# VectorE's order in two stages of a fused two-layer kernel: branch weights ahead of modulation products, and modulation products four steps earlier

## The chip, the cores and the metric

The kernel runs on one core of a Trainium2 chip. The metric is the device time of one execution in microseconds; the kernel before takes 3525.2 us in the median of 3 runs (3522.25 to 3526.55). A profiled execution stands beside them, and all times inside the kernel are from it.

## The reference

Two layers of different kinds follow each other on 1024 tokens of width 1024, in float32. Layer one: RMS norm, an input projection, neighbourhood attention, a recurrent branch with gates, a gated mix of the two branches, and an MLP with a squared ReLU. Layer two is a modulated layer with window attention and a gated delta rule; its norms are scaled and shifted by vectors that come from a small product:

```
# layer one, end
mixed = sigmoid(g_att) * y_att + sigmoid(g_rec) * y_rec      # y_att = att @ w_att_o, y_rec = rec @ w_rec_o
x = x + mixed @ w_out[l]
h2 = rms_norm(x, ln2_g[l])
x = x + square(relu(h2 @ w_ff1[l])) @ w_ff2[l]
x = rms_norm(x, lnf_g)
# layer two, start
mod   = silu(c)     @ w_ada + b_ada                           # w_ada: 1024 x 6144
mod_c = silu(c_ctx) @ w_ada + b_ada
sh1, sc1, gt1, sh2, sc2, gt2 = split(mod, 6)
h = rms_norm_2(x, g_norm1) * (1 + sc1) + sh1
```

The change touches only the computation of `mod` and `mod_c`, which depends on nothing in layer one and is therefore done beside layer one's work, and the weights of `y_att` and `y_rec`.

## The kernel before

Every engine runs a program written out by hand, and semaphores tie them. Nothing reorders the instructions: each engine takes them as they are written. Large products are done in three matmuls each, because an operand is held as a high half and a low half: ScalarE copies the high half (L954 for the branch weights, L472 for the gate weights, L1539 for the MLP entries), and VectorE subtracts it from the plain values to get the low half (L959, L477, L1543).

**Modulation.** w_ada is cut into 12 groups of 512 columns, each of 8 blocks of 128 rows. VectorE multiplies a block by the vector's values and adds it up (`vector_mod`: L1395 for the first block of a group, L1398 for the others); groups 0 to 3 are done for two vectors, so 16 instructions, the rest for one, so 8. TensorE then sums the partitions with matmuls of one column (`tensor_mod`, L1418), and VectorE adds the bias (`vector_mod_out`, L1405). Groups 0 to 7 lie in the gate stage, groups 8 to 11 in the down product of layer one's MLP.

**Gate stage (`tensor_mix1`, `scalar_mix1`, `vector_mix1`).** Sixteen jobs x; in pass x TensorE computes the gates of job x (two halves of 24 matmuls), then the branch product of job x-1, then the column sums of modulation group x-1 (for the first eight). ScalarE applies the tanh to the gates (L1020), then splits off the high half of the gate weights for the next job and of the branch weights for job x-1. VectorE, for job x: bias column, modulation products of group x, low half of the branch weights, then the two evacuations (L1107) with the low half of later gate weights (L477) between them. Loads of w_ada blocks go three deep through SyncE, in one queue with the weights.

**Down product (`tensor_ff7` from `ORDER7`, `vector_ff7`, `sync_ff7`).** Layer one's MLP is done as seven products in the way of Strassen. The second half has 7 products of 16 steps, 112 steps u; a step is 12 matmuls with one block of hidden rows and one block of weights. Both are entries split by ScalarE and VectorE (L1539, L1543) in a ring of eight, so these run at most four steps ahead. For each step VectorE takes, in this order: an evacuation of the product before (`vector_taken`, L2014), a sum of weights for two steps on (`total`, L1890), the two low halves, and `vector_between`, where `it` is u-4 and the modulation products stand. SyncE brings the hidden rows in blocks of four steps (`rows(r)`, block r for steps 4r to 4r+3, issued when VectorE has done the first low half of step 4r-5), the weight pieces (`stream`), the two loads of X that the evacuations add to, and w_ada in pairs of blocks through four places (`sync_mod_pair`, pair y for products 2y and 2y+1, counted from the first of group 8). From the fifth on, a pair is issued when the products have left its place. `MOD_AT` says before which step TensorE makes the column sums of which group.

Of the kernel before, what the change touches and what calls it, by code (L numbers as in the profile page):

```python
# [131 lines left out]
def build(nc, d, out):  # L132
    ctx = ExitStack()
    with ctx:
# [58 lines left out]
        def R(off, n):  # L193
            return A[:, off:off + n]
# [279 lines left out]
        def vector_weights(e, x):  # L474
            o = 2048 * (x % 2)
            e.wait_ge(*m2_hi.at(split_at(x)))
            e.tensor_tensor(RR[:, o:o + 1024], MG[x % 2], RR[:, o + 1024:o + 2048].bitcast(F32),  # L477
                            ALU.subtract).then_inc(*m2_lo.tick())
# [447 lines left out]
        def branch_place(x):  # L926

            if x < 8:
                o = 1024 * (x % 2)
                return 20480 + o, TMP[:, o:o + 512], 4  # L930
            return (20480, TMP[:, 0:1024], 8) if x % 2 == 0 else (47104, YD[:, 0:1024], 8)
# [24 lines left out]
        def vector_branch(e, x):  # L956
            o, raw, kt = branch_place(x)
            e.wait_ge(*yd_hi.at(x + 1))
            e.tensor_tensor(RR[:, o:o + kt * 128], raw, RR[:, o + kt * 128:o + kt * 256].bitcast(F32),  # L959
                            ALU.subtract).then_inc(*yd_lo.tick())  # L960
# [10 lines left out]
        def vector_rec_lo(e, h):  # L971
            c = slice(h * 512, h * 512 + 512)
            for kk in range(8):
                e.wait_ge(*h_hi.at(h_lo.n + 1))
                e.tensor_tensor(RCL[:, kk, c], RC(kk, c), RCH[:, kk, c].bitcast(F32), ALU.subtract).then_inc(*h_lo.tick())
# [72 lines left out]
        def vector_mixed_lo(e, i):  # L1048
            kk, h, cols = unit_tile(i)
            e.wait_ge(*h_hi.at(16 + i + 1))  # L1050
            e.tensor_tensor(MXL[:, kk, cols], mixed_in(0, kk, h), MXH[:, kk, cols].bitcast(F32),
                            ALU.subtract).then_inc(*h_lo.tick())
# [9 lines left out]
        def vector_outw(e, name, i):  # L1062
            raw, lo, hi = OUTW[name]
            e.wait_ge(*m2_hi.at(outw_at(name, i)))
            e.tensor_tensor(RR[:, lo + i * 1024:lo + i * 1024 + 1024], raw[:, i * 1024:i * 1024 + 1024],
                            RR[:, hi + i * 1024:hi + i * 1024 + 1024].bitcast(F32), ALU.subtract).then_inc(*m2_lo.tick())
# [15 lines left out]
        def vector_mix1(e):  # L1082
            for u in range(32):
                x, h = divmod(u, 2)
                tt = tmpx[u % len(tmpx)]
                key = ("mo",) + mixed(x, h)
                ps, c, m, h = key[1:]
                dst = mixed_in(ps, c * 4 + m, h)
                if h == 0 and x < 8:
                    if x:  # L1090
                        vector_mod_out(e, x - 1)
                    for z in range(8 * x, 8 * x + 8):
                        vector_mod(e, z)
                if u == 17:
                    vector_mod_out(e, 7)
                if h == 0 and x and x not in (8, 15):
                    vector_branch(e, x)
                if u == 29:
                    vector_branch(e, 15)
                for i in MIXED_LO.get(u, ()):  # L1100
                    vector_mixed_lo(e, i)
                if u == 30:
                    for i in range(4):
                        vector_outw(e, "wo0", i)
                e.wait_ge(*bk.full(key))
                e.wait_ge(*bk.clear(("mg",) + key[1:]))
                e.scalar_tensor_tensor(out=tt if ps % 2 else dst, in0=tt, scalar=1.0, in1=bk.tile(key)[:, :],  # L1107
                                       op0=ALU.add, op1=ALU.mult).then_inc(*bk.emptying(key))
                if h == 0 and x + 2 < 16:
                    vector_weights(e, 24 + x + 2)  # L1110
                if u == 15:
                    vector_rec_lo(e, 0)
                    vector_branch(e, 8)
                    vector_rec_lo(e, 1)
            for i in (14, 15):
                vector_mixed_lo(e, i)
# [234 lines left out]
        mod_rows = lambda g: 2 if g < 4 else 1  # L1351
        acc_of = lambda g, b: R(47104 + 512 * b, 512) if g < 8 else R(51200 + g % 2 * 512, 512)
        pair_place = lambda y: (20480, 21504, 49152, 50176)[y % 4]
        MOD_AT = {22: 8, 30: 9, 38: 10, 46: 11}

        def raw_of(z):
            if z < 64:
# [18 lines left out]
        def sync_mod_pair(e, y):  # L1376
            g, kk = divmod(64 + 2 * y, 8)
            if y >= 4:
                e.wait_ge(*m_part.at(64 + 2 * y - 6))
            elif y == 0:  # L1380
                e.wait_ge(*bk.clear(("m3", 0, 15)))
            e.dma_start(R(pair_place(y), 1024).rearrange("p (k n) -> p k n", k=2),
                        d["w_ada"][kk * 128:kk * 128 + 256, g * 512:g * 512 + 512].rearrange("(k p) n -> p k n", p=P)
                        ).then_inc(*l_x[y % 4].tick())

        def vector_mod(e, z):
            g, kk = divmod(z, 8)
            e.wait_ge(*raw_there(z))
            if kk == 0 and (1 <= g < 8 or g >= 10):
                e.wait_ge(*bk.full(("md", g - 1 if g < 8 else g - 2)))  # L1390
            for b in range(mod_rows(g)):
                acc, scale = acc_of(g, b), sc3[:, kk, b:b + 1]
                last = b == mod_rows(g) - 1
                if kk == 0:
                    ins = e.tensor_scalar(acc, raw_of(z), scale, None, ALU.mult)  # L1395
                else:
                    e.wait_ge(*(m_part if last else dv).now())
                    ins = e.scalar_tensor_tensor(out=acc, in0=raw_of(z), scalar=scale, in1=acc, op0=ALU.mult, op1=ALU.add)  # L1398
                ins.then_inc(*(m_part if last else dv).tick())

        def vector_mod_out(e, g):
            key = ("md", g)
            e.wait_ge(*bk.full(key))
            for b in range(mod_rows(g)):
                ins = e.tensor_tensor(mods[:, b * 48 + g * 4:b * 48 + g * 4 + 4], bk.tile(key)[:, b * 4:b * 4 + 4],  # L1405
                                      V("bada", g * 4, 4), ALU.add)
            ins.then_inc(*bk.emptying(key))
# [51 lines left out]
        def seven(blk):  # L1459
# [131 lines left out]
            def tensor_ff7(e):  # L1591
# [22 lines left out]
                for pi, i in enumerate(ORDER7):  # L1614
# [4 lines left out]
                    for kts, ts in groups:  # L1619
                        if blk == 0 and 16 * pi + kts[0] in MOD_AT:  # L1620
                            tensor_mod(e, MOD_AT[16 * pi + kts[0]])
                        for t in ts:
# [411 lines left out]
            def sync_ff7(e):  # L2034
# [78 lines left out]
                    keep(KEEP2, t)  # L2113
                for r in range(4, 28):
                    rows(r)
                    if blk == 0 and r == 4:
                        for y in range(4):
                            sync_mod_pair(e, y)
                    if r == 4:
                        for k in range(2):  # L2120
                            e.wait_ge(*hidden_out(14 + k))
                        for h in range(2):
                            e.dma_start(X[:, 4 * h:4 * h + 4, :], x_of(xs)[:, 4 * h:4 * h + 4, :]).then_inc(*l_x3[h].tick())
                    if r < 26 and ORDER7[(r + 2) // 4] in STREAMED:
                        stream(ORDER7[(r + 2) // 4], (r + 2) % 4)
                    if blk == 0 and 5 <= r < 11:
                        for y in (2 * r - 6, 2 * r - 5):
                            sync_mod_pair(e, y)
                    if blk == 0 and r == 15:
                        e.wait_ge(*bk.full(("md", 11)))  # L2130
                        e.dma_start(lnf, row("lnf")).then_inc(*l_lnf.tick())
                        e.dma_start(Cx, d["ctx_2"].rearrange("(t p) n -> p t n", p=P)).then_inc(*l_c.tick())
# [86 lines left out]
                                       op1=ALU.mult).then_inc(*z_x.tick())  # L2219

        def vector_between(e, it):
            if 12 <= it < 44:
                vector_mod(e, 64 + it - 12)
            if it in (25, 33, 41, 49):
                vector_mod_out(e, 8 + (it - 25) // 8)
            if it == 50:
                vector_gains(e)
            k = it - 96
            if k == 2:
                vector_norm_mean(e, "nc")  # L2230
            if k == 4:
                vector_norm_factor(e, "nc")
                vector_norm_rows(e, "nc", 2, 0)
            if k == 8:
                vector_last_mean(e, 0)
            if k in (10, 11):
                e.wait_ge(*f_sm.now())
                vector_last_rows(e, 0, range(2 * k - 20, 2 * k - 18))
# [1736 lines left out]
```

## Time and profile before

| | |
|---|---|
| median of 3 runs | 3525.2 us (3522.25 to 3526.55) |
| profiled execution | 3526.55 us, its span 3524.7 us |
| mean granted TensorE clock | 0.964 |
| TensorE busy | 3289.8 us, 93% of the span |
| VectorE busy | 2275.9 us, 65% |
| ScalarE busy | 1465.9 us, 42% |

A span is the time from the first to the last instruction. Engines are named PE (TensorE), DVE (VectorE), ACT (ScalarE), POOL (GpSimd) and SPq (SyncE's queue of DMA issues). A timeline row reads: start, length, engine, line, operation, what is written and read, the number of instructions merged into it, and in brackets how long the engine stood idle before it and what released it. The DMA's issue rows end with the time from issue to landing.

### The profile page before, as it was taken

To read this page: it belongs to the slowest core of one execution; us is meant where nothing else is said; L and a number is where in the kernel's file an instruction comes from. 1 tells how busy PE (TensorE), PEld (TensorE's weight loads), DVE (VectorE), ACT (ScalarE), POOL (GpSimd) and SP (SyncE) were. 2 spreads that over 40 slices of the span, in tenths; PEclk is the share of its full clock that TensorE was granted. 3 is DMA by queue.
4 is the path that set the end of the run, shared out by engine and by line. 5 is a ranking of instruction groups with operands and counts; after the bars stand their busy time and mean duration, and the time that the engine had idled before them with its cause. 6 is when DMAs were issued, how large, how long until landed. Compare 5 with 4: busy or idle time off the path is not lost. (4 is left out here: it accounts for less than half of the span.)

```text
span 3524.7 us, 49737 instructions
## 1 busy us (share of the span) xinstructions
PE 3289.8 (93%) x19066; PEld 2531.6 (72%) x19066; DVE 2275.9 (65%) x3919; ACT 1465.9 (42%) x2690; POOL 572.1 (16%) x377
## 2 busy tenths in 40 slices
PE   7999998999999999999985776999999999999999
PEld 6767777887778887776554665646788657888887
DVE  4176997513498858786567886459422149885887
ACT  3176771212355443354434554218411035544443
POOL 1081000011134420010000000105201123442000
PEclk9999999999999999999997887999999999999999
DMA  3101115413144486553002122300022313447454
GB/s 135 44 3 31 45 36 159 129 50 114 60 138 149 152 308 209 193 185 135 4 15 42 36 46 59 108 18 2 19 54 69 105 48 123 164 152 278 148 196 157
DMA packets 311173, 363.20 MB, mean 103 GB/s; under 512 B 68660, under 2 KB 218100, under 8 KB 306460
## 3 DMA queue, kind: packets, MB, share of 16 engines
q1 hardware_dynamic: 309180, 352.95, 30.1%
q10 hardware_dynamic: 1760, 7.08, 0.9%
q8 instruction: 154, 2.52, 0.3%
q14 instruction: 79, 0.65, 0.1%
HBM read 269.38 MB, written 88.77 MB: 102 GB/s over the span
## 5 line engine op out<-in xcount | busy, mean ns | idle before, releaser
L96 PE MATMUL ps<-halves 128*128 128x512 f32 x4304 | 1007.3, 394 | 14.5 <-DVE halves L403 5.2
L96 PEld LDWEIGHTS ps<-halves 128*128 128x128 f32 x4304 | 811.6, 190 | 189.1 <-issue 10.1
L1586 PE MATMUL ps<-halves 128*128 128x512 f32 x2736 | 630.0, 393 | 9.5 <-DVE halves L1687 7.4
L1632 PE MATMUL ps<-halves 128*128 128x512 f32 x2688 | 616.3, 391 | 9.2 <-DVE arena L2014 5.5
L1586 PEld LDWEIGHTS ps<-halves 128*128 128x128 f32 x2736 | 518.4, 190 | 120.5 <-DVE halves L1687 8.3
L1632 PEld LDWEIGHTS ps<-halves 128*128 128x128 f32 x2688 | 505.7, 189 | 117.9 <-DVE arena L2014 7.4
L1539 ACT ACTIVATE halves<-raws 128x512 fp32r<-128x512 f32 x324 | 202.1, 630 | 446.1 <-PE ps L1632 307.7
L1543 DVE TENSOR_TENSOR halves<-raws,halves 128x512 fp32r<-128x512 f32 x324 | 268.9, 840 | 126.9 <-ACT halves L1539 126.0
L96 PE MATMUL ps<-arena 128*128 128x512 f32 (+1 forms) x800 | 315.1, 554 | 4.7 <-ACT arena L2784 3.0
L96 PEld LDWEIGHTS ps<-arena 128*128 128x128 f32 x800 | 151.9, 191 | 161.3 <-issue 152.4
L96 PE MATMUL ps<-arena,tokens 128*128 128x512 f32 (+1 forms) x384 | 140.4, 523 | 0.3 <-DMA tokens<-h_stash 0.3
L695 POOL TENSOR_SCALAR arena<-arena,sm 128x512 f32<-128x512 f32 x64 | 99.4, 1566 | 149.5 <-DVE sm L660 149.5
L1020 ACT ACTIVATE arena<-ps,hb 128x512 f32<-128x512 f32 x32 | 21.9, 688 | 233.5 <-PE ps L96 224.6
L96 PEld LDWEIGHTS ps<-arena,tokens 128*128 128x128 f32 x384 | 72.5, 191 | 62.7 <-issue 59.3
L1543 DVE TENSOR_TENSOR halves<-down_sums,halves 128x512 fp32r<-128x512 f32 x160 | 109.5, 684 | 0.0
L1661 ACT ACTIVATE staged<-staged 128x512 f32<-128x512 f32 x124 | 76.8, 620 | 75.6 <-DVE staged L1805 32.0
L1239 DVE SCALAR_TENSOR_TENSOR arena<-arena,ps 128x512 f32<-128x512 f32 x32 | 22.0, 686 | 129.0 <-PE ps L96 128.7
L2885 DVE TENSOR_TENSOR arena<-arena 64x30 f32<-64x30 f32 (+5 forms) x300 | 98.4, 328 | 10.0
L2888 DVE TENSOR_TENSOR arena<-arena 64x30 f32<-64x30 f32 (+5 forms) x300 | 97.8, 326 | 10.3
L1539 ACT ACTIVATE halves<-down_sums 128x512 fp32r<-128x512 f32 x160 | 98.6, 616 | 0.4 <-DVE down_sums L1890 0.4
L2025 POOL TENSOR_TENSOR staged<-staged 128x512 f32<-128x512 f32 x32 | 42.2, 1317 | 333.5 <-ACT staged L1663 333.5
L3576 POOL TENSOR_SCALAR arena<-arena,wst 128x640 f32<-128x640 f32 (+1 forms) x32 | 74.9, 2342 | 113.1 <-DVE wst L3536 113.1
(371 smaller groups left out, 4440.8 us busy)
## 6 DMA issues: line engine op xcount, KB each, us to landing
hidden_rows<-staged SPq DMA_DIRECT2D x32, 1792.0 KB, 5.8
raws<-hidden_rows SPq DMA_DIRECT2D x56, 1024.0 KB, 5.2
mixw<-in_w_in SPq DMA_DIRECT2D x56, 512.0 KB, 3.9
arena<-in_w_ada SPq DMA_DIRECT2D x64, 256.0 KB, 2.9
raws<-in_w_ff SPq DMA_DIRECT2D x32, 512.0 KB, 5.3
arena<-in_w_ff SPq DMA_DIRECT2D x16, 1024.0 KB, 7.4
raws<-in_w_mlp SPq DMA_DIRECT2D x32, 512.0 KB, 5.5
arena<-in_w_mlp SPq DMA_DIRECT2D x16, 1024.0 KB, 7.4
```

The costliest lines, as they stand in the source:

```text
L96: ins = e.matmul(out_ap, l, r, start=i == 0, stop=i == n - 1)
L695: e.tensor_scalar(pbuf[i % 5], pbuf[i % 5], c[:, 2:3], None, ALU.mult).then_inc(*a_sl.tick())
L1239: e.scalar_tensor_tensor(out=tt if ps % 2 else dst, in0=tt, scalar=1.0, in1=bk.tile(key)[:, :], op0=ALU.add, op1=ALU.mult).then_inc(*bk.em ...
L1539: e.activation(entry_part(x, 0), entry_source(x), ACT.Copy).then_inc(*f_wh.tick())
L1543: e.tensor_tensor(entry_part(x, 1), entry_source(x), entry_part(x, 0).bitcast(F32), ALU.subtract).then_inc(*f_ws.tick())
L1586: ins = e.matmul(o[:, :], l[:, k, :], r[:, k, :], start=first and k == 0 and i == 0, stop=last and k == 3 and i == 2)
L1632: ins = e.matmul(banks[t][:, :], l, r, start=kt == 0 and j == 0, stop=kt == 15 and j == 2)
L1661: e.activation(dst, dst, ACT.Relu).then_inc(*f_fh.tick())
L2025: e.tensor_tensor(staged(n, 5), staged(n, 3), staged(n, 7), ALU.add).then_inc(*f_sq.tick())
L2885: e.tensor_tensor(T3, bc(W3[:, k:k + 1, k + 1:32], [64, k, 31 - k]), bc(W3[:, 0:k, k:k + 1], [64, k, 31 - k]), ALU.mult).then_inc(*dv.tick())
L2888: e.tensor_tensor(W3[:, 0:k, k + 1:32], W3[:, 0:k, k + 1:32], T3, ALU.add).then_inc(*(i_sol if k == 30 else dv).tick())
L3576: e.tensor_scalar(p, p, w4[i % 4][:, 6:7], None, ALU.mult).then_inc(*w_sl.tick())
```

## The change

Two edits. In `vector_mix1` the low half of the branch weights (`vector_branch`, L959) is taken before the bias column and the modulation products of its job. In the down product the modulation products, their column sums, the bias columns and the gains (`vector_gains`) stand four steps earlier, and SyncE's issue of the pairs is rearranged: none ahead of the loads of X, and two behind each of the row blocks 4 to 11.

```
@@ vector_mix1
+                if h == 0 and x and x not in (8, 15):
+                    vector_branch(e, x)
                 if h == 0 and x < 8:
                     if x:
                         vector_mod_out(e, x - 1)
                     for z in range(8 * x, 8 * x + 8):
                         vector_mod(e, z)
                 if u == 17:
                     vector_mod_out(e, 7)
-                if h == 0 and x and x not in (8, 15):
-                    vector_branch(e, x)
@@
-        MOD_AT = {22: 8, 30: 9, 38: 10, 46: 11}
+        MOD_AT = {18: 8, 26: 9, 34: 10, 42: 11}
@@ sync_ff7
                 for r in range(4, 28):
                     rows(r)
-                    if blk == 0 and r == 4:
-                        for y in range(4):
-                            sync_mod_pair(e, y)
                     if r == 4:
                         for k in range(2):
                             e.wait_ge(*hidden_out(14 + k))
...
-                    if blk == 0 and 5 <= r < 11:
-                        for y in (2 * r - 6, 2 * r - 5):
+                    if blk == 0 and 4 <= r < 12:
+                        for y in (2 * r - 8, 2 * r - 7):
                             sync_mod_pair(e, y)
@@ vector_between
-            if 12 <= it < 44:
-                vector_mod(e, 64 + it - 12)
-            if it in (25, 33, 41, 49):
-                vector_mod_out(e, 8 + (it - 25) // 8)
-            if it == 50:
+            if 8 <= it < 40:
+                vector_mod(e, 64 + it - 8)
+            if it in (21, 29, 37, 45):
+                vector_mod_out(e, 8 + (it - 21) // 8)
+            if it == 46:
                 vector_gains(e)
```

VectorE in the gate stage, around the products of group 1 (L1395 and L1398), between two evacuations (L1107):

```order
 L477 TENSOR_TENSOR halves<-mixw,halves 128x1024
 L1107 SCALAR_TENSOR_TENSOR valw<-arena,ps 128x512
+L959 TENSOR_TENSOR halves<-tmps,halves 128x512
 L1405 TENSOR_TENSOR mods<-ps,vec 128x4 x2
 L1395 TENSOR_SCALAR arena<-arena,sc 128x512 x2
 L1398 SCALAR_TENSOR_TENSOR arena<-arena,sc 128x512 x14
-L959 TENSOR_TENSOR halves<-tmps,halves 128x512
 L1107 SCALAR_TENSOR_TENSOR valw<-arena,ps 128x512
```

L959 moved over the bias column and sixteen products; the same happens in jobs 2 to 7.

SyncE in the down product, from the last weight piece that is kept; raws are the blocks of rows 4 and 5, arena<-x_stash the loads of X. Before:

```order
L2078 DMA kept<-in_w_ff 128x4x512 x2
L2061 DMA raws<-hidden_rows 128x4x512
L1382 DMA arena<-in_w_ada 128x2x512 x4
L2123 DMA arena<-x_stash 128x4x1024 x2
L2061 DMA raws<-hidden_rows 128x4x512
L1382 DMA arena<-in_w_ada 128x2x512 x2
```

And now, where L2120 is the line that was L2123:

```order
L2078 DMA kept<-in_w_ff 128x4x512 x2
L2061 DMA raws<-hidden_rows 128x4x512
L2120 DMA arena<-x_stash 128x4x1024 x2
L1382 DMA arena<-in_w_ada 128x2x512 x2
L2061 DMA raws<-hidden_rows 128x4x512
L1382 DMA arena<-in_w_ada 128x2x512 x2
```

The first two pairs moved behind the loads of X, and the next two behind row block 5.

TensorE at the first column sums of the down product (L1418; L1632 are its steps, 12 matmuls each):

```order
 L1572 MATMUL ps<-identm,arena 128x128 x32
 L1586 MATMUL ps<-halves 128x512 x1320
-L1632 MATMUL ps<-halves 128x512 x264
+L1632 MATMUL ps<-halves 128x512 x216
 L1418 MATMUL ps<-onec,arena 128x1 x4
 L1632 MATMUL ps<-halves 128x512 x96
```

They moved from behind 22 steps to behind 18.

## Rows read from the trace of the kernel before

**Rows 1.** The page, busy time and share of the span by engine.
```profile
PE 3289.8 (93%) x19066; PEld 2531.6 (72%) x19066; DVE 2275.9 (65%) x3919; ACT 1465.9 (42%) x2690; POOL 572.1 (16%) x377
```

**Rows 2.** The timeline of TensorE in the gate stage.
```profile
571.30 1.84 PE L1418 MATMUL ps<-onec,arena 128*128 128x1 f32 x16
573.00 11.19 PE L96 MATMUL ps<-halves 128*128 128x512 f32 x48
...
592.30 11.19 PE L96 MATMUL ps<-halves 128*128 128x512 f32 x48
...
628.70 16.63 PE L96 MATMUL ps<-halves 128*128 128x512 f32 x72
...
645.98 16.63 PE L96 MATMUL ps<-halves 128*128 128x512 f32 x72
```

**Rows 3.** The waits of 515 to 850 us (total, times, longest).
```profile
PE ps L96 <- DVE halves L959: 1.6, 2, 0.9
```

**Rows 4.** The timeline of VectorE in the gate stage.
```profile
553.31 0.87 DVE L1395 TENSOR_SCALAR arena<-arena,sc 128x512 f32<-128x512 f32 x2
...
564.05 0.69 DVE L959 TENSOR_TENSOR halves<-tmps,halves 128x512 fp32r<-128x512 f32 x1
568.78 0.69 DVE L1107 SCALAR_TENSOR_TENSOR valw<-arena,ps 128x512 f32<-128x512 f32 x1 [4.04 <-PE ps L96]
...
628.96 0.49 DVE L1395 TENSOR_SCALAR arena<-arena,sc 128x512 f32<-128x512 f32 x1
...
637.84 0.69 DVE L959 TENSOR_TENSOR halves<-tmps,halves 128x512 fp32r<-128x512 f32 x1
```

**Rows 5.** The timeline of ScalarE in the gate stage.
```profile
562.16 0.62 ACT L954 ACTIVATE halves<-tmps 128x512 fp32r<-128x512 f32 x1
...
580.32 0.62 ACT L954 ACTIVATE halves<-tmps 128x512 fp32r<-128x512 f32 x1
```

**Rows 6.** The timeline of TensorE, the first twenty down steps.
```profile
1269.04 54.56 PE L1632 MATMUL ps<-halves 128*128 128x512 f32 x240
```

**Rows 7.** The timeline of VectorE in down steps 12, 16 and 20.
```profile
1296.36 0.68 DVE L1543 TENSOR_TENSOR halves<-kept,halves 128x512 fp32r<-128x512 f32 x1
...
1306.47 0.48 DVE L1395 TENSOR_SCALAR arena<-arena,sc 128x512 f32<-128x512 f32 x1
...
1319.64 0.69 DVE L2014 TENSOR_TENSOR arena<-arena,ps 128x512 f32<-128x512 f32 x1 [4.25 <-DMA arena<-x_stash]
```

**Rows 8.** Windows: length, busy (count) per engine, PEclk, DMA share, GB/s.
```profile
543.30:557.00 13.70, 7.42 (x26) 6.58 (x27) 12.01 (x21) 0.07 (x1) 0.00 (x0) 0.50 0.63 186
...
1366.00:1369.40 3.40, 3.40 (x8) 2.22 (x9) 1.90 (x3) 0.26 (x1) 0.00 (x0) 0.50 0.97 354
...
1293.00:1320.00 27.00, 27.00 (x121) 22.36 (x120) 13.11 (x21) 9.24 (x16) 0.00 (x0) 1.00 1.04 396
```

**Rows 9.** The timeline of TensorE, around three waits and column sums.
```profile
1332.47 1.02 PE L1418 MATMUL ps<-onec,arena 128*128 128x1 f32 x8 [2.38 <-DVE arena L1398]
...
1365.87 17.02 PE L1632 MATMUL ps<-halves 128*128 128x512 f32 x66 [2.75 <-DVE arena L2014]
...
1405.45 0.94 PE L1418 MATMUL ps<-onec,arena 128*128 128x1 f32 x8
```

**Rows 10.** The timeline of SyncE's queue in row block 4.
```profile
1292.80 5.55 SPq L1382 DMA_DIRECT2D arena<-in_w_ada  x4
1298.45 3.80 SPq L2123 DMA_DIRECT2D arena<-x_stash  x2
```

**Rows 11.** DMA issues at 1292.8 and at 1299.8 (KB, us to landing).
```profile
arena<-in_w_ada SPq DMA_DIRECT2D x1, 512.0 KB, 11.7
...
arena<-x_stash SPq DMA_DIRECT2D x1, 2048.0 KB, 19.8
```

**Rows 12.** DMA issues of 1320 to 1430 us (KB, median us to landing).
```profile
raws<-hidden_rows SPq DMA_DIRECT2D x9, 1024.0 KB, 6.0
...
arena<-in_w_ada SPq DMA_DIRECT2D x10, 512.0 KB, 3.9
```

## The prediction

> **What bounds the kernel now.** I read the page first: TensorE is busy for 93% of the span [rows 1], so nearly all that makes it wait is added to the end, and what runs beside it is free until it makes it wait. Then I read the timelines of two stretches, engine against engine, because the edit moves VectorE work in both: the gate stage (16 passes, 540 to 860 us) and the first block's down product (from 1269 us).
>
> In the gate stage TensorE's pass is 48 matmuls of gates, 24 of the branch product (twice as many from the ninth branch on) and the column sums of the modulation (L1418). The timeline shows gates starting at 573.00 and 592.30, a pass of 19.3 us while products have two rows, and at 628.70 and 645.98, 17.28 us, once they have one [rows 2]. The view of waits has TensorE waiting twice for the low half of the branch weights (L959), 1.6 us in all [rows 3]. VectorE has room: behind its products and L959 it stands idle for 4.0 us until the branch product is full [rows 4].
>
> The reader should see one more thing there. ScalarE makes the high half of the branch weights (L954) behind its tanh, and that tanh waits for the gates of the *next* pass: with gates from 573.00, L954 runs from 580.32 to 580.94, 7.9 us into TensorE's pass [rows 2, 5]. VectorE's products fill just these 8 us today.
>
> In the down product a step is 12 matmuls; 20 steps take 54.56 us, 2.73 each [rows 6]. The step numbers on VectorE come from its first product, L1395 at 1306.47, which belongs to step 16; four pairs of L1543 earlier, the one that ends at 1297.04 is step 12's [rows 7]. VectorE runs at most four steps ahead of TensorE, as an entry's slot is free only when the entry eight back is used.
>
> **Part 1: L959 ahead of the products.** It removes two TensorE waits, 1.6 us. It moves one instruction of 0.69 us over 9 or 17 others, and with it a wait: VectorE executes in order, so the bias column (L1405), the products and all behind them (evacuation L1107, weight halves L477) now stand behind ScalarE's L954.
> Pass x=1: L954 ends at 562.78 [rows 5]; L959 takes 0.7, L1405 0.15 and the 16 products, 553.31 to 564.05, 10.7 [rows 4]: they end at 574.3. The column sums that began at 571.30 [rows 2] begin at 574.4: +3.1 us.
> Passes x=2 and 3: counted from the gates' start, the products end at 7.9 + 0.7 + 0.15 + 10.8 = 19.6. Then come 1.7 us of column sums, and beside them L1107 (0.6) and L477 (1.2), which the next gates need: 21.5 against 19.3, +2.2 each, +4.4.
> Passes x=4 to 7: eight products take 8.9 (628.96 to 637.84) [rows 4]; 7.9 + 0.7 + 0.1 + 8.9 = 17.6, and L1107, L477 and 0.1 of latency make 19.5 against 17.28: +2.25 each, +9.0.
> The plain waits sum to 16.5 us, the 1.6 saved already inside. The loads of w_ada are issued as products free their places, so they move with them and the groups keep their length.
>
> To this comes TensorE's clock. The windows show it full (1.00, that is 2.4 GHz) while TensorE works without a gap, and half (0.50, 1.2 GHz) over 543.3 to 557.0, where it had stopped for the first products [rows 8]. The 2.75 us wait before 1365.87 is followed by 3.4 us at 0.50, in which 1.7 us are lost; the 2.38 us wait before 1332.47 is followed by no such stretch [rows 8, 9]. A two-row pass would now hold 3 us of wait and 1.7 of column sums of one column each; a one-row pass 1.1 of wait, 0.8 of sums and 1 more of wait. Bounds for a pass: 0 and 1.7 us. I take the drop after all three of the first kind and half of the other four, 5 x 1.7 = 8.5, less 1 that falls into waits: 7.5. Part 1 comes to +24 us. The Trainium skill (TensorE: Matmul & The Clock Gate, What's actually happening) says that the throttled state is the default and activity releases it. Read strictly, all seven passes would pay, 12 us in place of 7.5. The trace agrees that a stop is paid for afterwards, but it has one wait that costs and one that doesn't.
>
> **Part 2: modulation products four steps earlier.** VectorE's work is unchanged: 32 products of 0.66 us in steps 12 to 43, where they stood in 16 to 47. Steps 44 to 47 become 0.66 us lighter, where TensorE doesn't wait; the 2.75 us wait in step 32 is for evacuations (L2014) whose place is unchanged, and stays [rows 9]. So the move brings little by itself, and what counts is when the data are there. SyncE now issues both 2 MB loads of X first and behind them two w_ada pairs in place of four ahead of them; later, the pair for step 4r-4 goes out right behind block r of rows, and that one when VectorE has done the first subtraction of step 4r-5. The pair thus leaves one step before its use, where it was seven or more.
>
> The first pair: from 1293 to 1320 the DMAs move 396 GB/s with all engines busy [rows 8], 2.6 us for 1 MB, and they land in the order of issue: the pair issued at 1292.80 takes 11.7 us (1304.5), the last load of X, issued at 1299.8, takes 19.8 (1319.6), where VectorE goes on [rows 7, 10, 11]. Of these 6 MB, 5 now stand up to the second pair's end: it lands at 1317.0, the first at 1315.7. Bounds: 1304.5, its landing now, and 1319.6, behind everything; I take 1315.7 for the order seen. TensorE ends step 12 at 1304.5 (1269.04 + 13 x 2.73), and step 13's halves are ready at 1315.7 + 0.4 + 1.2 = 1317.3: it waits 12.8 us.
>
> Then come turns of four steps. From the issue of the rows to the landing of the pair behind them: a pair lands in 3.9 us in the median, 1 MB ahead of it adds 2.6: 6.5 us. Bounds 3.9 (not held up) and 7.3 (the rows' own median 6.0 and 1.3 for the half MB) [rows 12]. Blocks 10 and 11 have a 1 MB weight piece between: 9.1. From the landing to the next issue VectorE does its product (0.66), two steps (a pair of L1543 1.2, a product 0.66, with an evacuation or sum another 0.6) and the third's head: 5.0 us with pairs and products alone, 6.8 with the 0.6 in each. TensorE's four steps take 10.9.
> So from 1315.7: +4.7 = 1320.4, where block 5 leaves; +6.5 + 5.0 = 1331.9; twice +6.5 + 6.8 = 1358.5; +6.5 + 6.0 = 1371.0; +6.5 + 6.8 = 1384.3; +9.1 + 6.8 = 1400.2; +9.1 and 8.0 for the last four products = 1417.3. There the last column sums can start, ahead of step 42. Today they start at 1405.45 ahead of step 46 [rows 9], so step 42 began at about 1394.5. That is +23 us; the 2.38 us that TensorE now loses before 1332.47 lies inside. Drops of the clock after the long waits at steps 13 and 32, less those of before, add 1: +24 us.
>
> The Trainium skill (DMA: Bandwidth & Descriptors, Two DMAs through the same engine are not ordered) says that nothing orders DMAs across the 16 engines. If small pairs overtook the 2 MB loads here, the first rival below would hold. The landings seen don't show it: they come in the order of issue.
>
> **Sum.** 24 + 24 = 48 us on the profiled execution of 3526.55 us (span 3524.7). The median of the runs lies 1.35 lower: 3525.2 + 48 = 3573 us. Nothing later that I found starts at a fixed time, so I let nothing be given back.
>
> **Rivals.**
> *The data come in time; part 1 alone.* The first pair lands at 1304.5 and the others in 3.9 us. Then TensorE waits 1.6 us at step 13, a turn is 3.9 + 6.8 = 10.7, just under its 10.9, and part of the 2.38 us goes: about 0, and 3525 + 24 = 3549 us. For it: the 3.9 us row. Against: each pair stands behind at least 1 MB.
> *Slack covers part 1; part 2 alone.* If L954 were ready 3 us earlier, the products would end when TensorE arrives; 3549 us again. Against it: L954 follows the gates in both passes shown.
> *Faster, as it looks on paper.* L959 no longer holds TensorE (-1.6), and products one turn earlier end the 2.38 us wait: 3521 us. It is decided at one point in each part: L954 must be there when VectorE reaches it (553.3 in pass 1, and it is 9.5 us later), and the first pair by 1297.04.
> *SyncE's queue.* With full rings four w_ada issues took 5.55 us [rows 10]. If each of 7 turns pays 2 us for issuing, that adds 14, and the clock drops in all seven passes, +4: 3591 us.
>
> **Numbers.** The forecast has 62%, part 1 alone 12%, part 2 alone 8%, the queue 9%, faster 5%, and gains and losses that cancel 4%, of which 3 stay within 0.2% (7 us, about what a measurement of this kernel can tell). If the forecast's case holds I expect 3560 to 3588; eight in ten reach down to the two rivals at 3549: 3548 to 3590. Slower is 62 + 12 + 8 + 9 + 1 = 92%, same 3%, faster 5%.
>
> **What would show it.** Part 1: VectorE idle for 8 to 10 us before each L959, released by L954; TensorE waits of about 3 us (three times) and 1 us before L1418; gates 19.5 to 21.5 us apart, more where 0.50 is granted. Part 2: VectorE idle 18 us before L1395 of step 12, released by a w_ada load; TensorE 12 us before step 13; then waits of 3 to 5 us for w_ada in every fourth step. The gate stage ends 24 us later, step 48 of the down product 48 us later. Wrong would be passes still 17.3 us apart (part 1), or L1395 of step 12 without a long wait (part 2).

## The result and the profile after

The changed kernel takes 3603.53 us in the median (4 runs, 3600.57 to 3605.43), against 3523.98 (4 runs, 3522.25 to 3526.55) for the kernel before: a ratio of 1.0224, 95% interval [1.0207, 1.0242]. It is slower by 79 us. Its profiled execution has a span of 3603.3 us and a mean granted clock of 0.952, against 3524.7 and 0.964.

All of the loss lies in the two stretches of the prediction. The tenth-pass gates start 37.4 us later than before (717.91 against 680.52), the down product starts 38.1 later (1307.16 against 1269.04), and the bank wait in its step 48 ends 80.4 later (1495.82 against 1415.44). After that the lag stays near that. So the gate stage costs about 37 us and the down product 42.

**Gate stage.** VectorE in the changed kernel, passes 1 and 2 (start, length, line, idle before it and releaser), which answers to [rows 4]:

```profile
565.47 0.69 DVE L959 TENSOR_TENSOR halves<-tmps,halves 128x512 fp32r<-128x512 f32 x1 [11.80 <-ACT halves L954]
566.08 0.22 DVE L1405 TENSOR_TENSOR mods<-ps,vec 128x4 f32<-128x4 f32 x2
...
577.29 0.68 DVE L1107 SCALAR_TENSOR_TENSOR valw<-arena,ps 128x512 f32<-128x512 f32 x1
...
590.49 0.69 DVE L959 TENSOR_TENSOR halves<-tmps,halves 128x512 fp32r<-128x512 f32 x1 [10.79 <-ACT halves L954]
```

L959 now stands where it was put, and VectorE idles 8.8 to 12.0 us before each of the seven, behind ScalarE's L954. L1107 follows its products without a gap, where it idled 4.04 us in [rows 4]: the slack is used up, and TensorE pays. TensorE in the same stage, which answers to [rows 2]:

```profile
577.52 3.48 PE L1418 MATMUL ps<-onec,arena 128*128 128x1 f32 x16 [3.39 <-DVE arena L1398]
580.86 18.29 PE L96 MATMUL ps<-halves 128*128 128x512 f32 x72
602.20 3.54 PE L1418 MATMUL ps<-onec,arena 128*128 128x1 f32 x16 [3.05 <-DVE arena L1398]
605.60 19.45 PE L96 MATMUL ps<-halves 128*128 128x512 f32 x72
...
672.20 1.02 PE L1418 MATMUL ps<-onec,arena 128*128 128x1 f32 x8 [1.04 <-DVE arena L1398]
673.93 19.45 PE L96 MATMUL ps<-halves 128*128 128x512 f32 x72 [0.71 <-DVE halves L477]
```

Two things are to be seen. The waits are those foreseen: 3.05 to 3.39 us with two rows, 1.04 to 1.79 and then 0.71 for L477 with one. And 72 matmuls take 17.9 to 19.5 us, where they took 16.63 in [rows 2]; the sixteen column sums take 3.0 to 3.5 in place of 1.84. The matmuls themselves are slower. The waits view of 540 to 720 us (total, times, longest) and the windows of the seven passes (start:end, length, then busy time and count of PE, PEld, DVE, ACT and POOL, granted clock, DMA share, GB/s) give both sums. The first window is of the kernel before, the second of the changed one:

```profile
DVE halves L959 <- ACT halves L954: 73.6, 7, 12.0
...
PE ps L1418 <- DVE arena L1398: 15.2, 7, 3.4
...
PE ps L96 <- DVE halves L477: 2.8, 4, 0.7
```

```profile
552.99:680.52 127.53, 125.96 (x585) 104.73 (x586) 77.09 (x119) 20.54 (x30) 0.00 (x0) 0.98 0.51 151
```

```profile
554.85:717.91 163.06, 145.04 (x585) 118.48 (x586) 75.31 (x119) 23.39 (x35) 0.00 (x0) 0.87 0.41 121
```

TensorE's waits are 15.2 + 2.8 = 18.0 us, less the 1.6 that went [rows 3]: 16.4 more. The seven passes take 163.1 us where they took 127.5 (552.99 to 680.52), 35.5 more. The other 19.1 us are slower matmuls: TensorE is busy for 145.04 us with the work that took 125.96. The granted clock is 0.87, so for about 42 us of the stage it is at its lower level (1.2 GHz), where at 0.98 before it was for about 5. (The last 1.9 of the 37.4 us were there before the edit can act: the sums of group 0 start at 551.44 in place of 549.58.) Two of the passes by themselves, one with two rows and one with one:

```profile
580.86:605.60 24.74, 21.69 (x90) 18.05 (x90) 13.62 (x22) 2.84 (x4) 0.00 (x0) 0.84 0.40 120
...
653.24:673.93 20.69, 18.94 (x81) 15.40 (x81) 8.75 (x14) 2.84 (x4) 0.00 (x0) 0.91 0.46 138
```

**Down product.** VectorE at steps 12, 16, 20 and 21, and TensorE, which answer to [rows 7] and [rows 9]:

```profile
1353.65 0.49 DVE L1395 TENSOR_SCALAR arena<-arena,sc 128x512 f32<-128x512 f32 x1 [18.52 <-DMA arena<-in_w_ada]
...
1365.04 0.75 DVE L1398 SCALAR_TENSOR_TENSOR arena<-arena,sc 128x512 f32<-128x512 f32 x1 [4.11 <-DMA arena<-in_w_ada]
...
1376.62 0.49 DVE L1395 TENSOR_SCALAR arena<-arena,sc 128x512 f32<-128x512 f32 x1 [3.42 <-DMA arena<-in_w_ada]
1377.02 0.68 DVE L2014 TENSOR_TENSOR arena<-arena,ps 128x512 f32<-128x512 f32 x1
```

```profile
1355.40 15.68 PE L1632 MATMUL ps<-halves 128*128 128x512 f32 x60 [12.71 <-DVE halves L1543]
1377.76 1.87 PE L1418 MATMUL ps<-onec,arena 128*128 128x1 f32 x8 [6.68 <-DVE arena L2014]
...
1404.37 1.02 PE L1418 MATMUL ps<-onec,arena 128*128 128x1 f32 x8 [1.12 <-DVE arena L1398]
...
1431.71 7.34 PE L1632 MATMUL ps<-halves 128*128 128x512 f32 x18 [8.50 <-DVE arena L2014]
1443.94 1.86 PE L1418 MATMUL ps<-onec,arena 128*128 128x1 f32 x8 [4.88 <-DVE arena L2014]
```

The late data are there as forecast: 18.52 us of VectorE, 12.71 of TensorE, then 4.11 four steps on. New is the releaser of two column sums. Before steps 18 and 34 TensorE waits 6.68 and 4.88 us, not for the products (L1398) but for an evacuation (L2014): the sums before step 18 start at 1377.76, as VectorE ends its evacuation of step 21, which itself stood behind a late w_ada pair (3.42 us). The waits view of 1307 to 1496 us has it in sum:

```profile
PE ps L1632 <- DVE halves L1543: 12.7, 1, 12.7
PE ps L1418 <- DVE arena L2014: 11.6, 2, 6.7
PE ps L1632 <- DVE arena L2014: 10.6, 2, 8.5
PE ps L1418 <- DVE arena L1398: 3.9, 2, 2.7
```

That is 38.8 us of waits against 7.9 before. With 42.3 us lost in the stretch, 11.4 are left for the clock; the granted clock is 0.88 there, against 0.99 before.

### The profile page after: what moved, and what is told of

Same layout as the page of the kernel before. It is cut to its first block and busy times, and to the rows that moved or that the text cites. A ratio compares the mean times of both kernels' runs of the same rounds, so it can differ in the third digit from the quotient of the medians.

```text
span 3603.3 us, 49737 instructions
## 1 busy us (share of the span) xinstructions
PE 3325.8 (92%) x19066; PEld 2557.2 (71%) x19066; DVE 2273.1 (63%) x3919; ACT 1466.1 (41%) x2690; POOL 571.2 (16%) x377
## 5 line engine op out<-in xcount | busy, mean ns | idle before, releaser
L96 PE MATMUL ps<-halves 128*128 128x512 f32 x4304 | 1022.4, 399 | 14.4 <-DVE halves L403 5.1
L96 PEld LDWEIGHTS ps<-halves 128*128 128x128 f32 x4304 | 823.2, 192 | 192.7 <-issue 10.7
L1632 PE MATMUL ps<-halves 128*128 128x512 f32 x2688 | 626.8, 396 | 26.3 <-DVE halves L1543 15.8
L1586 PE MATMUL ps<-halves 128*128 128x512 f32 x2736 | 629.7, 393 | 9.4 <-DVE halves L1687 7.6
L1632 PEld LDWEIGHTS ps<-halves 128*128 128x128 f32 x2688 | 513.2, 191 | 138.1 <-DVE halves L1543 17.7
L1586 PEld LDWEIGHTS ps<-halves 128*128 128x128 f32 x2736 | 518.4, 190 | 120.2 <-DVE halves L1687 8.5
L1398 DVE SCALAR_TENSOR_TENSOR arena<-arena,sc 128x512 f32<-128x512 f32 x112 | 80.7, 747 | 34.3 <-DMA arena<-in_w_ada 32.4
```

The costliest lines, as they stand in the source:

```text
L96: ins = e.matmul(out_ap, l, r, start=i == 0, stop=i == n - 1)
L1586: ins = e.matmul(o[:, :], l[:, k, :], r[:, k, :], start=first and k == 0 and i == 0, stop=last and k == 3 and i == 2)
L1632: ins = e.matmul(banks[t][:, :], l, r, start=kt == 0 and j == 0, stop=kt == 15 and j == 2)
```

## The experiments

Each is timed against the kernel before on the same chip. Two theories were at stake. A: each part costs by itself, and what was missed in part 1 is TensorE's clock. B: what was missed in part 2 is that a column sum takes a bank of PSUM, where TensorE's results lie until another engine has evacuated them. The rivals are named with each.

**Each part alone.** `p1_only` has the edit in `vector_mix1`, `p2_only` all the others.

> Part 1 alone: L959 ahead of the products, the down product as before. Theory A (each part costs by itself, and what was missed in part 1 is TensorE's clock): +37 us against before, about 3561, with the seven passes 21 to 26 us long as in the changed kernel. Rival (the prediction's own size of part 1, the rest comes from part 2 or from both together): +24 us, 3548.

Measured 3564.06 us, ratio 1.0113 [1.0098, 1.0128], 40 us over before. That is theory A's 37 within 3 us; the predicted 24 is ruled out. The waits are as in the changed kernel (14.8 and 2.1 us for L1398 and L477).

> Part 2 alone: products, column sums, bias, gains and loads of the down product as in the changed kernel, the gate stage as before. Theory A: +42 us, about 3566. Rival: the prediction's own size, +24 us, 3548.

Measured 3565.85 us, ratio 1.0116 [1.0101, 1.0131], 42 us over. The two losses, 40 and 42, add to 81, against the 79 measured for both, so there is next to nothing between the parts.

**The releaser of L959.** `p1_high_first` has part 1, and ScalarE's half moved as well:

```
 scalar_mix1
+                if h == 0 and 2 <= x <= 8:
+                    scalar_branch(e, x - 1)
                 e.wait_ge(*bk.full(key))          # the gates of pass x, then the tanh
...
-                    elif x >= 2:
+                    elif x > 9:
                         scalar_branch(e, x - 1)
```

> Part 1 with ScalarE's half moved too: L954 of job x-1 stands before the wait for the gates of pass x, for jobs 1 to 7. Theory A (part 1 costs because L959 stands behind an L954 that follows the next pass's gates): L959 finds its data, the passes are back at 19.0 and 17.3 us, and the two waits for L959 are gone: 3522, 2 us under before. Rival (it is the place of L959 on VectorE that costs, or the loads of w_ada): the passes stay above 20 us, +37 us.

Measured 3525.37 us, ratio 0.9995 [0.9985, 1.0004]. The 40 us are gone with one ScalarE instruction moved, so L959's place costs only through L954. The waits for L959 are gone too, and the two-row passes are shorter than before:

```profile
592.28 1.84 PE L1420 MATMUL ps<-onec,arena 128*128 128x1 f32 x16
593.98 16.63 PE L96 MATMUL ps<-halves 128*128 128x512 f32 x72
610.45 1.84 PE L1420 MATMUL ps<-onec,arena 128*128 128x1 f32 x16
```

Column sums to column sums is 18.2 us, no wait in it (L1420 is L1418 in this file). The whole stage from the first column sums to the gates of pass 9 is 129.84 us against 130.94 before; 1 us is less than the run can show, and the 3522 us expected did not come.

**The clock.** `p1_filled` is part 1 with work for TensorE while it would wait, on operands that it has and into the bank that the sums overwrite:

```
 tensor_mod(e, g)
             e.wait_ge(*bk.vacant(key))
+            for i in range(0 if g < 1 or g > 7 else 12 if g < 4 else 5):
+                e.matmul(o[:, :], H1H[:, i % 8, 0:128], H1H[:, i % 8, 0:512], start=True, stop=True)
             e.wait_ge(*m_part.at(8 * g + 8))
```

> Part 1 alone, and TensorE does extra matmuls of 512 columns (12 before the column sums of groups 1 to 3, 5 before those of groups 4 to 7) into the bank that the sums overwrite, while it would wait for the products. Theory A (half of part 1's cost is the lowered clock behind the waits): the granted clock stays 1.00 in most passes, they shrink to about 21.8 and 19.6 us, and the time is +18 to +24 us, about 3545, although TensorE has more to do. Rival (the passes are long because VectorE's own chain is): no gain, +37 us or more, 3561 to 3570.

Measured 3547.01 us, ratio 1.0064 [1.0047, 1.0081]: 56 matmuls more, and 17 us less than part 1 alone (still 22 over before). The windows of the seven passes, part 1 alone and filled:

```profile
554.75:715.77 161.02, 143.97 (x586) 118.11 (x586) 75.31 (x119) 23.36 (x35) 0.00 (x0) 0.87 0.42 123
```

```profile
553.62:705.10 151.48, 145.63 (x641) 119.31 (x642) 75.33 (x119) 22.87 (x34) 0.00 (x0) 0.95 0.44 130
```

TensorE at the second filled stop (L1414 are the fillers, L1420 the column sums):

```profile
594.44 2.88 PE L1414 MATMUL ps<-halves 128*128 128x512 f32 x12
598.56 1.95 PE L1420 MATMUL ps<-onec,arena 128*128 128x1 f32 x16 [1.23 <-DVE arena L1398]
```

The clock goes from 0.87 to 0.95 and 9.5 us go in this window. The time in which TensorE does nothing useful has not shrunk: 13.8 us of fillers and 5.8 of waits, where part 1 alone waits for 17.0. But the useful matmuls take 131.8 us in place of 144.0. VectorE's work is the same (75.31 and 75.33 us). It reaches its products sooner, because the gates before them are quicker. About 3 more are saved outside it up to the next long wait (for L1051, which ends at 873.42 against 886.21); the rest lies later and is not explained. So the clock, not only the wait, is what the stops cost. It did not stay at 1.00: two-row passes are 22.4 to 23.2 us where 21.8 was expected, one-row passes 19.6 to 21.0.

**Column sums and their bank.** `p2_sums_late` keeps the column sums, bias and gains of before:

```
 p2_only -> p2_sums_late
-        MOD_AT = {18: 8, 26: 9, 34: 10, 42: 11}
+        MOD_AT = {22: 8, 30: 9, 38: 10, 46: 11}
-            if it in (21, 29, 37, 45):  ... if it == 46:
+            if it in (25, 33, 41, 49):  ... if it == 50:
```

> As part 2 alone, but the column sums stay before steps 22, 30, 38 and 46, with bias and gains where they were; products and loads are early. Theory B (what the prediction missed in part 2 is that early column sums take a PSUM bank that an evacuation, L2014, of step 21 or 38 must free first): the waits of TensorE for L2014 before L1418 vanish, and what is left is the late data, +19 to +24 us, about 3545. Rival (the data explain all of part 2): as part 2 alone, about 3566.

Measured 3549.12 us, ratio 1.0069 [1.0052, 1.0086], +25. No column sum waits any more, and the data waits are unchanged (12.60 us at step 13, 28.4 + 16.6 us of VectorE for w_ada). So 17 of the 42 us hang on where the sums (with bias and gains) stand, and 25 on the data. Of the 25, 7 show up in step 32, where TensorE's wait for L2014 has grown from 2.75 to 9.69 us:

```profile
1389.43 18.24 PE L1632 MATMUL ps<-halves 128*128 128x512 f32 x66 [9.69 <-DVE arena L2014]
```

**The data.** `p2_loads_early` leaves `sync_ff7` as it was before and has the rest of part 2.

> As part 2 alone, but the w_ada pairs are issued where they were (four ahead of the loads of X, then two per block of rows). Theory B: the waits for data fall from 12.7 to under 2 us at step 13 and to none later, but TensorE still waits for L2014 before the column sums of steps 18 and 34: +10 to +18 us, about 3538. Rival (data explain all): within 3 us of before, 3524.

Measured 3534.66 us, ratio 1.0028 [1.0018, 1.0038], +10. TensorE, with its two waits for L2014 ahead of column sums:

```profile
1302.30 13.89 PE L1632 MATMUL ps<-halves 128*128 128x512 f32 x60 [1.67 <-DVE halves L1543]
1321.49 1.87 PE L1418 MATMUL ps<-onec,arena 128*128 128x1 f32 x8 [5.30 <-DVE arena L2014]
...
1368.65 6.06 PE L1632 MATMUL ps<-halves 128*128 128x512 f32 x18 [2.75 <-DVE arena L2014]
1378.03 1.25 PE L1418 MATMUL ps<-onec,arena 128*128 128x1 f32 x8 [3.31 <-DVE arena L2014]
```

The data wait at step 13 is 1.67 us, the bank waits of 5.30 and 3.31 are still there. The wait in step 32 is at 2.75 us again, so it was the late data that lengthened it. Data and bank cost 25 and 10 singly and 42 together. Of the last 7 the waits explain a part: with both, TensorE waits 11.9 us for L2014 ahead of column sums in place of 8.6, as VectorE, held up by data, reaches the freeing evacuation later, and 3.8 us for products (L1398), which neither has alone. No run takes the two apart further.

`p2_sums_at_20` differs from it in one line, `MOD_AT = {20: 8, 28: 9, 36: 10, 44: 11}`.

> As the one with early loads (products four steps earlier, w_ada pairs issued where they were, bias and gains four steps earlier), but the column sums only two steps earlier: before steps 20, 28, 36 and 44 in place of 18, 26, 34 and 42. Theory B (the bank is freed by VectorE's evacuation of step 21, which VectorE reaches while TensorE is at step 17 to 19): the wait for L2014 before the first and third column sums falls from 5.3 and 3.3 us to under 1.5 us each, and the time from +10 us to between -3 and +3, about 3523. Rival (any early column sum costs, because the products' end moves with the work before it): the waits stay, 3530 or more.

Measured 3520.29 us, ratio 0.9988 [0.9979, 0.9997]. Two steps later, the same column sums wait for nothing:

```profile
1302.89 19.33 PE L1632 MATMUL ps<-halves 128*128 128x512 f32 x84 [1.63 <-DVE halves L1543]
1322.17 1.05 PE L1418 MATMUL ps<-onec,arena 128*128 128x1 f32 x8
```

Two steps, 5.5 us of TensorE's work, turn +10 into -5: theory B. (It had said between -3 and +3.)

**The move without what came with it.** `p2_products_only` changes only the two lines of `vector_between` that call `vector_mod`.

> Only VectorE's products of the down product four steps earlier; loads, column sums, bias and gains as before. Theory B: neither the data wait (first pair lands 7.5 us after VectorE wants it, but TensorE is 7.5 us behind) nor the bank wait is there, and the 2.38 us wait before the first column sums goes: 3521 to 3524. Rival (early products load VectorE and delay the entries): +5 us or more.

Measured 3521.72 us, ratio 0.9991 [0.9982, 1.0]. VectorE's products four steps earlier cost nothing. Whether the kernel is faster by 3 us can't be said, only that it is not slower.

**A version meant to be faster.** `group0_later` is `p1_high_first` with the sums of group 0 moved, to take away the stop ahead of them (9.37 us before 549.58 in the kernel before):

```
 tensor_mix1
                         tensor_gate(e, 24 + x, ("mg",) + mixed(x, h), h, x_ea)
+                        if (x, h) == (2, 0):
+                            tensor_mod(e, 0)
...
-                if j < 8:
+                if 1 <= j < 8:
                     tensor_mod(e, j)
 vector_mix1
                         vector_mod(e, z)
+                        if z == 3:
+                            vector_weights(e, 26)
...
-                if h == 0 and x + 2 < 16:
+                if h == 0 and 0 < x < 14:
                     vector_weights(e, 24 + x + 2)
 MOD_AT = {24: 8, 30: 9, 38: 10, 46: 11}
```

> A version meant to be faster than both: L954 and L959 early as in the one before; the column sums of group 0 between the two gate halves of pass 2, with the low half of that pass's weights (L477) taken in the middle of group 0's products; first column sums of the down product before step 24. It takes away TensorE's stop of 9.4 us before group 0's sums and the half clock behind it. Theory A and B: 8 us of wait, 2 to 4 of clock, 1.6 of L959 and 2.4 of step 22 go: 3510 to 3514. Rival (another wait comes in at once, VectorE being as far behind): 3520 to 3524.

Measured 3513.9 us, ratio 0.9965 [0.9952, 0.9978]: 11 us under the kernel before. Its profiled execution is the fastest of the five, at 3507.05. TensorE:

```profile
543.65 7.99 PE L96 MATMUL ps<-halves 128*128 128x512 f32 x24 [5.12 <-DVE halves L477]
551.48 1.84 PE L1424 MATMUL ps<-onec,arena 128*128 128x1 f32 x16
553.18 11.19 PE L96 MATMUL ps<-halves 128*128 128x512 f32 x48
```

The stop is 5.12 us in place of 9.37, so it is not gone, and it now ends with gates in place of sums (L1424 is L1418 here). Gates of pass 3 start at 566.37, where they started at 573.00.

> The faster version with the down product's products four steps earlier and its column sums back before step 22, all loads where they were: it joins two changes that each came out at or under the time before. If they add, 3 us under the faster version, about 3510 to 3512. Rival (both remove the same wait at step 22): equal to it, 3514.

It is `group0_later` with the products of `p2_products_only` and `MOD_AT` back at 22. Measured 3514.73 us, ratio 0.9970 [0.9959, 0.9982]: equal. The two do not add. Both mend the 2.38 us wait at step 22, and the joint version has a wait of 1.68 us at step 13 that the other has not.

## Why the prediction was wrong

The direction was right, and so were the wait for L954 and the late data; a third mechanism, the bank, was missing. Three rivals (part 1 alone, part 2 alone, faster) are ruled out by the two single parts, which cost 40 and 42 us. The fourth, SyncE's queue, would have added 2 us of issuing to each turn, but in the turns of four steps the issues of a pair took 1.0 to 1.4 us, and with the sums left in place part 2 cost 25 and not 38. The slow issues of [rows 10] are seen again where the engines are saturated (5.20 us for the two of the first pair); whether a ring was full there, no run shows. The range ended at 3590, and 3603.5 lies outside. 48 us were forecast, 79 came. Step by step:

- *Plain waits of part 1, 16.5 us.* The trace has 16.4, and it comes out pass by pass (9.6 us of two-row and 8.4 of one-row waits, where the forecast has about 9 of each). L954 was the releaser, and moving it took the 40 us away.
- *The clock in part 1, 7.5 us.* This term failed: it was put at less than half. It measured 19.1 in the changed kernel. I took one drop of 1.7 us for a two-row pass and half a drop for the others from one row of a 2.75 us wait. But a two-row stop is 3 us of wait and then sixteen matmuls of one column, which themselves took 3.5 us once the clock had fallen. Its windows show 0.83 to 0.84 over whole passes of 25 us, which makes 8 us at the lower level, where the stretch behind the 2.75 us wait was 3.4. The one-row passes show 0.86 to 0.91. And the slower gates stand on the chain to L954, so each drop is paid in full. The filled waits, with 0.95 and 17 us less, show the term at work. The strict reading of the Trainium skill (TensorE: Matmul & The Clock Gate, What's actually happening), that the clock is lowered unless activity releases it, gave 12 and was the nearer one. The trace agrees: all seven passes are below 0.92.
- *Data of part 2, +24 us.* The terms came out: 18.5 us of VectorE against 18.7 for the first pair, 12.7 of TensorE against 12.8, 2.8 to 5.7 us waits in every fourth step, and with the sums left in place +25 us as a whole. Reckoned from the start of the down product, VectorE takes the pairs of steps 12, 16 and 20 within 0.2 us of the forecast. The pair of step 40 comes 3.3 us after its forecast with the sums left in place, but 17.5 after it in the changed kernel: TensorE's stops for the bank hold VectorE back, and VectorE the next issue. The landings kept the order of issue: the pair behind the X loads landed 18.5 us after its issue, at 1353.65, and the last load of X at about 1352.3.
- *The end of the chain.* "There the last column sums can start" was the step that failed in part 2. It let a column sum wait for its products alone. `tensor_mod` first opens a bank of the ring of eight, and for the sums before step 18 that is the bank of the first down product's first tile, which VectorE evacuates in its steps 20 and 21 (it ends at 1377.70). TensorE stops at step 17 until then. Before, the sums stood before step 22, where this was done. The order of the column sums was in the change; I moved them with their products and did not ask what their place takes. Leaving the sums (with bias and gains) in place takes away 17 us, and the two runs that differ in `MOD_AT` alone show it at 15 (+10 and -5).
- *Step 32.* I said the wait of 2.75 us "is for evacuations (L2014) whose place is unchanged, and stays". It became 8.5: the place is unchanged on VectorE, but VectorE came to it late. The forecast of 24 for the data holds as a whole because it was read off the end of VectorE's chain; where on the way TensorE would pay was wrong.
- *The clock in part 2, 1 us.* 11.4 us of the stretch are not waits. I had reckoned with drops behind the stops at steps 13 and 32 alone; there were stops at seven places.

What stays open: where the rest of the 17 us of the filled version beyond 12 to 13 comes from; how the 17 us of the sums' place split into bank waits, waits for products and clock; and why the stop ahead of the first column sums, the same code in all but the last two runs, ends between 546.8 and 551.7 in different executions.

## What to carry to other kernels

Before an instruction is moved ahead on an in-order engine, look at what releases it *now* and when: if that comes from the other engine's next pass, everything it passes inherits the wait. A moved step takes along every resource that it opens, not only its inputs; ask which bank, slot or queue place it needs and who frees it. A stop of the matmul engine has a second price in the clock behind it. Where a loop of 21 to 26 us repeated it, that price was as much as the wait itself (19.1 us on 16.4); in the down product it was over a third (11.4 on 30.9).

## What the runs showed of the hardware

Useless matmuls made a kernel faster: 56 of them, put into waits, took 17 us off 3564 (to 3547, with 3524 for the kernel that has no such waits). A pass of 25 us with a stop of 3 us and sixteen one-column matmuls behind it had a mean clock of 0.83 to 0.84; passes of 20.7 to 22.3 us with stops of 1.0 to 1.8 and 0.7 us around eight such matmuls had 0.86 to 0.91. Stops of 2.38 us and 1.63 to 1.67 us, alone in full work, left no mark that I found. While the DMA engines were saturated, 512 KB behind two loads of 2 MB landed 18.5 us after their issue; the same size took 3.9 us in the median later on [rows 12].
